# A hybrid decoder step on one core: first input chunk sent earlier, value rows and pooling maps interleaved anew, copy parts moved, last expert in pieces

## The reference

```
h = rms(x); q, k, v, u = split(h @ w_in)          # 12 heads x 64 each, u has 1280 channels
attn = dilated window attention(q, k, v, caches)  # samples read a window cache of 2048 rows
pool = (trailing mean of u over 2/4/8/16 rows - u) @ pool_w, scaled
x += concat(attn, pool) @ w_out
x += cross_attention(rms(x) @ w_cq, memory keys and values) @ w_co
group = top1(rms(x) @ w_rg + b_rg); experts = top2 of the group's 8 (w_re, b_re)
x += sum over the 2 experts: gate * ((silu(h @ w_e_gate) * (h @ w_e_up)) @ w_e_down)
```

## Time and profile before

| | us |
|---|---|
| median of 3 runs (lowest, highest) | 1586.22 (1583.8, 1587.32) |
| the profiled execution | 1590.57 |
| its span in the trace | 1588.7 |
| TensorE busy | 1260.9 |
| VectorE busy | 501.4 |
| ScalarE busy | 193.5 |
| bytes moved by DMA | 608.83 MB, 383 GB/s over the span |
| chain that ended last | DMA 50%, TensorE 43%, VectorE 3% |

### The profile page before, as it was taken

The page is one execution under the profiler, slowest core; times in us unless marked ns, Lnnn a source line. Parts: engine busy times, 40 slices in busy tenths (PEclk is TensorE's granted clock), DMA queues, the critical chain, the costliest instruction groups (busy, mean ns, idle before and its releaser), DMA issues.

```text
span 1588.7 us, 23505 instructions
## 1 busy us (share of the span) xinstructions
PE 1260.9 (79%) x10063; PEld 654.6 (41%) x10063; DVE 501.4 (32%) x1042; ACT 193.5 (12%) x464; POOL 59.6 (4%) x111
## 2 busy tenths in 40 slices
PE   7969999998999989676777677677677676676675
PEld 4434458773887866322222222222222222222222
DVE  2300155740000342442332332332332332332333
ACT  3200012320111134100000000000000000000000
POOL 2000012212000000000000000000000000000000
PEclk9989999997899999899889899899898998999898
DMA  9999999979899885699999999999999999999996
GB/s 358 339 370 332 331 348 375 390 226 366 308 395 407 333 339 216 285 398 426 425 427 428 424 428 426 424 427 427 424 428 428 423 429 426 424 429 426 426 427 259
DMA packets 113181, 608.83 MB, mean 383 GB/s; under 512 B 11118, under 2 KB 14341, under 8 KB 78681
## 3 DMA queue, kind: packets, MB, share of 16 engines
q1 hardware_dynamic: 71243, 479.10, 73.1%
q10 hardware_dynamic: 34486, 100.73, 17.4%
q0 software_dynamic: 7408, 28.37, 5.0%
HBM read 603.16 MB, written 106.18 MB: 446 GB/s over the span
## 4 chain that ended last, share of the span: by engine, by line
DMA 50%; PE 43%; DVE 3%; issue 2%; SPq 1%; ACT 1%; POOL 0%; DVEq 0%; ACTq 0%
DMA ring<-in_w_e_up_dram 44%; PE pb L1108 11%; PE pb L642 10%; PE pb L881 6%; DMA ring<-in_w_in_dram 3%; PE pb L728 2%; PE pb L1008 2%; PE pb L899 2%; PE pb L670 2%; DMA ring<-in_w_cq_dram 2%; PE pb L849 1%; PE pb L648 1%; DMA ring<-Z 1%; SPq L486 1%; PE pb L859 1%
## 5 line engine op out<-in xcount | busy, mean ns | idle before, releaser
L1108 PE MATMUL pb<-ring,xT 128*32 128x256 f32 x4096 | 312.4, 473 | 198.6 <-DMA ring<-in_w_e_up_dram 197.8
L1108 PEld LDWEIGHTS pb<-ring,xT 128*32 128x32 f32 x4096 | 155.2, 134 | 378.9 <-DMA ring<-in_w_e_up_dram 245.4
L1948 DVE TENSOR_TENSOR Z<-pb,Z 128x512 f32<-128x512 f32 x256 | 158.4, 680 | 343.8 <-PE pb L1072 343.8
L642 PE MATMUL pb<-ring,hreg 128*128 128x512 f32 (+1 forms) x320 | 127.4, 558 | 13.9 <-issue 13.9
L1135 PE MATMUL pb<-ring,xT 128*32 128x512 f32 x992 | 113.9, 600 | 0.0
L1072 PE MATMUL pb<-xT 32*128 32x512 f32 (+1 forms) x768 | 106.2, 623 | 3.7 <-DVE Z L1948 2.6
L1048 PE MATMUL pb<-Z,xT 128*32 128x512 f32 (+1 forms) x768 | 95.3, 610 | 3.0 <-DVE xT L1926 3.0
L642 PEld LDWEIGHTS pb<-ring,hreg 128*128 128x128 f32 x320 | 61.1, 193 | 77.1 <-issue 75.4
L881 PE MATMUL pb<-hreg,ring 128*128 128x264 f32 x320 | 78.1, 402 | 2.8 <-DMA ring<-in_w_out_dram 2.8
L728 PE MATMUL pb<-hreg,ring 128*128 128x264 f32 x320 | 76.2, 398 | 5.1 <-DMA ring<-in_w_in_dram 5.1
L1450 ACT ACTIVATE xT<-pb 128x128 f32<-128x128 f32 x32 | 8.9, 277 | 526.8 <-PE pb L1108 526.8
(11 more groups left out here) (323 smaller groups left out, 1122.6 us busy)
## 6 DMA issues: line engine op xcount, KB each, us to landing
ring<-in_w_e_gate_dram SPq DMA_DIRECT2D x64, 2048.0 KB, 19.0
ring<-in_w_e_up_dram SPq DMA_DIRECT2D x64, 2048.0 KB, 23.5
ring<-in_w_e_down_dram SPq DMA_DIRECT2D x31, 4096.0 KB, 22.1
out_win_k_sample_dram<-in_cache_win_k_dram ACTq DMA_DIRECT2D x24, 1536.0 KB, 12.9
out_win_v_sample_dram<-in_cache_win_v_dram ACTq DMA_DIRECT2D x24, 1536.0 KB, 14.9
ring<-in_w_in_dram SPq DMA_DIRECT2D x7, 4096.0 KB, 30.8
ring<-in_w_out_dram SPq DMA_DIRECT2D x4, 4096.0 KB, 32.1
out_win_k_sample_dram<-in_cache_win_k_dram ACTq DMA_DIRECT2D x8, 1488.0 KB, 14.9
```

Of the source, the lines that this page charges most:

```text
L642: last = mm(bk[:, 0:n], xt[:, k, tile * P:tile * P + P], w[:, k, 0:n], start=(k == 0), stop=(k == KT - 1))
L1108: last = mm(pb[1][32 * c:32 * c + 32, 0:256], XT[:, k % 4, 32 * (k // 4):32 * (k // 4) + 32], w[:, :, k8, P * c:P * c + P], start=(k == 0) ...
L1948: last = V.tensor_tensor(d, banks[c][:, :], d, ALU.add)
```

## The change

- SyncE sends the first chunk of w_in before it waits for the bias rows, not behind the load of their table.
- TensorE: the small matmuls on the pooling state come before the last channel tile (`channels(9)`), not behind it; the last channel rows are turned behind the first sample's value matmuls. The maps stand in front of the value matmuls of samples 1 to 7, two of them before 3, 4 and 6, where one stood behind each sample and two at the end. VectorE waits for the turned rows where it writes over the last two tiles.
- ScalarE: five copy parts fewer ahead of the output projection (one before the first input chunk, one each at the second and third, one at the last channel tile, one at the maps), the others at the maps later; one more in cross attention, one more in the last projection, and three behind the last exponential of the routing.
- The last expert: the second half of gate and up is loaded as two quarters, down as four (by column half, then by inner half); TensorE starts each when its piece is there. The down product goes to two banks by column half, each is copied and added to x by itself, and SyncE stores each piece of the prompt when it is final. ScalarE stores the sample rows. The branch for more blocks stands before the last expert.

```diff
+            big(IN0)
             sp.wait_ge(v_freed, v_at("bias", 0))
             sp.dma_start(bias_dram[:, :], brow[0:H, :]).then_inc(brow_stored, 16)
...
-            big(IN0)
             big(IN0 + 1)
...
-            with sp.Fori(2, NE) as i:
+            with sp.Fori(2, NE - 1) as i:
                 expert_weights(i, i)
+            sp.wait_ge(gu_used[0], NE - 1)
+            gate_up(NE - 1, NE - 1, 0)
+            sp.wait_ge(gu_used[1], NE - 1)
+            for q in range(2):
+                for m in range(2):
+                    src = a[("w_e_gate", "w_e_up")[m]][0][NE - 1].rearrange("(p k) n -> p k n", k=KT)
+                    at = 4096 * m + 2048 * q
+                    sp.dma_start(ring[:, 1, at:at + 2048].rearrange("p (k n) -> p k n", k=4), src[:, 8 + 4 * q:12 + 4 * q, :])\
+                        .then_inc(gu_landed[1] if q else quarter_landed, 16)
+            sp.wait_ge(dn_used, NE - 1)
+            w = a["w_e_down"][0][NE - 1].rearrange("(k p) n -> p k n", p=P)
+            for q in range(4):
+                c, f = slice(1024 * (q // 2), 1024 * (q // 2) + 1024), slice(2 * (q % 2), 2 * (q % 2) + 2)
+                sp.dma_start(slot2.rearrange("p (k n) -> p k n", k=4)[:, f, c], w[:, f, c]).then_inc(last_landed[q], 16)
...
+            for n, t, hf in ((1, 0, 0), (2, 1, 0), (3, 0, 1), (5, 1, 1)):
+                c = slice(1024 * hf, 1024 * hf + 1024)
+                sp.wait_ge(x_final, n)
+                sp.dma_start(a["y_prompt"][0, t * P:(t + 1) * P, c], x3[:, t, c]).then_inc(stored, 16)
...
-            channels(9)
-            channel_rows(8, 10)
...
-            piece_landed(pe, POOLW)
             pe.wait_ge(state_landed, 16)
...
+            channels(9)
...
+            sample_values(0)
+            channel_rows(8, 10)
+            piece_landed(pe, POOLW)
+            kt = 0
+            for b in range(1, NB):
+                for _ in range(2 if b in (3, 4, 6) else 1):
+                    pool_map(kt)
+                    kt += 1
+                sample_values(b)
...
+            def results(hf):
+
+                for t in ((0, 1), (0, 2, 1))[hf]:
+                    if t == 2:
+                        pe.wait_ge(x_final, 1)
+                    for c in range(4) if t == 2 else (2 * hf, 2 * hf + 1):
+                        r = slice(32 * c, 32 * c + 32)
+                        out = (pb[4 + c][:, :], pb[c][:, :], pb[4][32 * c:32 * c + NB, :])[t]
+                        last = mm(out, GT[r, slice(P * t, P * t + P) if t < 2 else slice(SEQ, TOK)], yo[r, :], start=True, stop=True)
+                    last.then_inc(out_filled, 1)
...
-            cache_part(3)
+            cache_part(2)
...
-                cache_part((2, 3, 3, 1, 0)[n])
+                cache_part((2, 2, 2, 1, 0)[n])
...
-                if o in (0,5,10):
+                if o in (0, 3, 6, 9):
                     cache_part()
...
+            cache_part(3)
+            assert parts == 8 * NB, parts
...
+                act.wait_ge(dn_used, NE)
+                nc.scalar.copy(yo[0:64, :], pb[3][0:64, :]).then_inc(yo_ready, 1)
+                act.wait_ge(dn_used, NE + 1)
+                nc.scalar.copy(yo[64:P, :], pb[2][64:P, :]).then_inc(yo_ready, 1)
+            act.wait_ge(x_final, 4)
+            for c in range(4):
+                act.dma_start(a["y_sample"][:, 0, 512 * c:512 * c + 512], x3s[32 * c:32 * c + NB, :]).then_inc(stored, 16)
```

More of the change, by code:

```diff
@@ L851, in pool_map, with sample_values @@
                 last.then_inc(a_filled, 1)
-            pe.wait_ge(a_freed, a_at("sturn", 1))
             sv = vbank("svals")
-            for b in range(NB):
+            def sample_values(b):
                 val_ready(pe, b)
@@ L1263, in channels @@
                 if j not in (0, 6):
[L1264 removed]
+                    cache_part()
             def channel_rows(first, end):
@@ L1436, in _ @@
             rows_back(3)
-            assert parts == 8 * NB, parts
             act.wait_ge(exp_in, 1)
@@ L1456, in expert @@
                 nc.scalar.copy(GT, pb[2][:, 0:TOK]).then_inc(gt_ready, 1)
-                act.wait_ge(dn_used, i + 1)
-                nc.scalar.copy(yo, pb[3][:, :]).then_inc(yo_ready, 1)
+                if not last_of_all:
+                    block_out(i)
             rows_out(0)
@@ L1948, in add_results, with results @@
                     last = V.tensor_tensor(d, banks[c][:, :], d, ALU.add)
-                    if final and c == 1:
-                        last.then_inc(x_final, 1)
-                last.then_inc(x_final if final else y_added, 1)
+                last.then_inc(y_added, 1)
+            def results():
+                for n, (hf, t) in enumerate(((0, 0), (0, 1), (1, 0), (1, 2), (1, 1))):
+                    dve.wait_ge(out_filled, n + 1)
+                    if t == 2:
+                        last = V.tensor_tensor(x3s, pb[4][:, :], x3s, ALU.add)
+                    for c in (2 * hf, 2 * hf + 1) if t < 2 else ():
+                        d = x3[:, t, 512 * c:512 * c + 512]
+                        last = V.tensor_tensor(d, pb[c if t else 4 + c][:, :], d, ALU.add)
+                    last.then_inc(x_final, 1)
             def expert(i, last_of_all=False):
@@ L1984, in _ @@
             n_over = dve.value_load(ov_i[0:1, OVB:OVB + 1], min_val=0, max_val=OVB)
-            expert(NE - 1, last_of_all=True)
             with dve.If(n_over > 0):
-                choose(NE)
-                rows_in(NE)
-                with dve.Fori(NE, NBLK) as i:
+                with dve.Fori(NE - 1, NBLK) as i:
                     expert(i)
-                for t in range(3):
-                    add_results(NBLK, t, pb[0:4] if t == 1 else pb[4:8], final=True)
             with dve.Else():
-                for t in range(3):
-                    add_results(NE, t, pb[0:4] if t == 1 else pb[4:8], final=True)
+                expert(NE - 1, last_of_all=True)
+            results()
 _INS = ['x_prompt', 'x_sample', 'cache_win_k', 'cache_win_v', 'state_pool', 'cache_mem_k', 'cache_mem_v', 'mem_prompt',
```

108 lines of the change are left out of this document (64 added, 44 removed).

## The result

| | before | changed |
|---|---|---|
| median of 4 runs each (lowest, highest) | 1585.01 (1583.3, 1587.32) | 1569.09 (1560.86, 1574.13) |
| the profiled execution | 1590.57 | 1574.13 |
| its span | 1588.7 | 1572.3 |

A forecast was written before the change was run, and what follows sets the result against it. Expert stage bound by bytes, mostly TensorE with four holes ahead of it. Gains 16.0 + 13.5 − 1.0 + 9.5 = 38.0 us take the profiled 1590.57 to 1552.6, the median from 1586.22 to 1548.2; range for 8 in 10: 1539 to 1566.

The forecast's parts named there:

- The early gain: First w_in chunk sent ahead of the bias rows, removing TensorE's wait: 16.0 us gained, bounds 7.7 and 16.0.
- covered, but with nothing to spare: Second w_in chunk: sent no earlier than 85, needed about 117, leaving 32 us, where w_out chunks land in 32.1.
- rival A: Early wait comes back at the second input chunk or the slowest one: 16 us lost, total 1564; chance 0.13.
- The middle: Value rows and pooling maps woven differently, removing waits and low-clock time: 13.5 us gained, bounds 5.6 and 19.4.
- B: Clock stays low in the woven stage: 9 us lost instead of 13.5 gained, total 1571; chance 0.11.
- D: Output projection starves as w_out chunks and w_cq meet a full queue: 59.6 us lost, total 1608; chance 0.05.
- a condition for the rest: Five copy parts fewer before the output projection free 18.3 us of engines, so the shortened stretch fits: 37 against 29.5.
- Routing: Three copy parts behind the last exponential, ending at 657 near the experts' first loads: 1.0 us lost, bounds 0 and 11.0.
- One sign of failure: The forecast fails as a whole if the expert loads start later than 645; they were expected near 629.
- The tail: Last expert loaded and finished in pieces: 9.5 us gained; lower bound the 1.9 of sample stores, upper 11.
- C's fixed cost: Last expert's smaller loads, 10 for 5, each pay about 2.0 us in series: total gain 28.5, time 1558; chance 0.08.
- The sum: Whole kernel: 16.0 + 13.5 − 1.0 + 9.5 = 38.0 us gained, for a median of 1548.2.

The follow-up runs named there:

- three profiles: The unaltered changed kernel, profiled once in each of three groups of runs; spans 1572.3, 1552.1 and 1569.9 us.
- second profile: The changed kernel again, unaltered, on another chip: span 1552.1 us; its group's median 1562.71 beside 1590.92 for the kernel before.
- first profile: The unaltered changed kernel as first measured: profiled execution 1574.13 us, span 1572.3; median 1569.09 beside 1585.01 for the kernel before.
- the third: The changed kernel once more, unaltered, on its own chip: span 1569.9 us; its group's median 1569.73 beside 1587.19 for the kernel before.
- the old order: TensorE's value rows and maps as before: in the changed kernel, median 1566.94 us; also in the kernel before with only w_in's first chunk moved ahead, 1579.97.
- the three groups: Runs of the unaltered changed kernel beside the kernel before: medians 1569.09 against 1585.01, 1562.71 against 1590.92, 1569.73 against 1587.19 us.
- parts behind the table: The changed kernel, with two of ScalarE's copy parts waiting until the bias table has landed: median 1557.49 us, ratio 0.9780 to the kernel before.
- three edits: The changed kernel with two copy parts waiting for the bias table, four parts later and the last down quarter before the first results: median 1558.26 us, ratio 0.9809.
- the first edit alone: The kernel before with only the first w_in chunk moved ahead of the bias rows: median of twelve 1579.97 us beside 1588.61, ratio 0.9949.

## Why the prediction was right or wrong

**The early gain, 16.0 predicted, is the step that failed.** It was 2.2, 16.3 and 5.8 in the three profiles and 11.6 between medians. The first chunk came out as forecast in the three. (The kernel before was profiled only at the lower level, 0.55 from 53 to 60 us; 2.2 and 5.8 compare the upper level with it, 16.3 like with like.) The step that failed is the one on what is moved past: "covered, but with nothing to spare". I took 32 us for the second chunk from w_out chunks, and called the store and the table covered since the table isn't needed for 60 us. But the store's 30.6 us hold back the table, and the table is what stands ahead of the second chunk in the queue. When the two leave decides how they fare against two copy parts, and the chunk took 46.2, 31.8 and 42.5 us in the three profiles. Nor does it hold that the chunk can't go before 85: it went at 83.0 and 81.9 at the upper level, yet landed later. With "nothing to spare" in the text, rival A should have had near half of the chance, not 0.13, and the range more room above. A's number, 1564, is near the three medians, but it has the 16 us lost always and to full engines; they are lost in some executions and kept in others.

**The middle, 13.5 predicted.** The stretch from the first value matmul to the first output tile took 51.4 us, and 40.4, 38.0 and 38.4 now: 11.1 to 13.5 less. The low clock behind the last values is gone (0.94 over the second profile's stretch), and B did not come as a whole: in the first profile 18 map records took 8.49 us at 371.0, at a clock of 0.51 from 371 to 379, where the second has 4.74. Two waits over 2 us stay, 2.31 in the second profile and 2.24 in the third, before the last value matmuls. D did not come: from the first output tile to w_cq it took 131.4, 129.3 and 131.4 us, 129.0 before. But the old order took 46.7 and 43.3 in two other profiles, so some 5 to 8 us of it are what that one execution had drawn; between means (47.1 of three profiles, 38.9 of the changed kernel's three) the order gives 8.2. That the gain against that one execution is near 13.5 is in part luck. The parts moved away carry another 9.2 between medians, which the prediction had as a condition for the rest and gave no price.

**Between the output projection and the experts** nothing was predicted to be lost. The second profile loses 1.2 us there; the first 4.3 (16.7 to 12.4), in w_cq's load (TensorE waits 6.03 us before its first use, 0.54 before the change) and in matmuls behind it at the lower level: 16.41 us for the first 64 records where before and the quickest profiles have 14.5.

**Routing, −1.0 predicted.** The lead shrinks by 0.7, 0.3 and 1.3 us from expert 0 to expert 1. That is right: the parts, with full engines from 639 to 651 us where before had none at 651, still run into the first loads. One sign of failure came true all the same: the first profile's flood of expert loads starts at 646.1, past the 645 that the prediction set (627.8 in the second, 643.8 in the third; 658.4 before).

**The tail, 9.5 predicted, 5.9 measured** (4.8 in the first profile). The answer to the earlier trace rows there; the first row is what stands behind the last gate and up matmuls:

```profile
1552.07 2.11 PE L1090 MATMUL pb<-xT 32*128 32x512 f32 x16
...
1555.64 3.66 PE L1116 MATMUL pb<-ring,xT 128*32 128x512 f32 x24
1560.04 1.99 PE L1110 MATMUL pb<-xT 32*128 32x512 f32 x8 [0.73 <-ACT xT L1525]
1561.96 1.91 PE L1116 MATMUL pb<-ring,xT 128*32 128x512 f32 x8
1564.55 3.16 PE L1110 MATMUL pb<-xT 32*128 32x512 f32 x16 [0.68 <-ACT xT L1527]
```

```profile
1563.91 0.58 ACT L1527 COPY xT<-pb 64x512 f32<-64x512 f32 x1 [4.02 <-PE pb L1116]
```

I put the copy of the second half 8.0 us behind the gate and up matmuls (1563.3 to 1571.3); it comes 11.8 behind (1552.1 to 1563.9). From it to the end I had 7.6, and it is 8.4. These 4.6 us are what is missing in this profile. The quarter is in TensorE's list behind the first results and their wait for the copy, 2.7 us that I had let run beside it. C's fixed cost is not seen: no wait of TensorE for a piece is over 1.4 us. The 2.0 us of the Trainium skill (DMA: Bandwidth & Descriptors, Anatomy of one DMA) are stated there for the path of GpSimd; SyncE issues these pieces, and no run here measures that cost.

**The sum.** For an execution in which the table leads, 36.6 against 38.0, and that by luck in part: the tail is 3 short, and the old kernel's profile was a poor one in the middle. For the median, 15.9, 28.2 and 17.5 in the three groups. With the order fixed it is 32.9 (parts behind the table) and 28.9 (three edits), so the race looks like the larger part of what is missing in the first and third group, and not all of it. That the other runs of the unaltered kernel split as their profiled ones do is inferred; they have no profile. The 3.2 us that the prediction took as what a measurement can tell were too small: the changed kernel's runs lie 13 to 21 us apart. Why the clock from 53 to 60 us falls now on one level and now on the other, and why the kernel before itself spreads over more than 20 us in each later group, stays open.

## What to carry to other kernels

A small store whose confirmation something waits for can take as long as what stands ahead of it in its queue: before moving a large load forward, follow every DMA that it is moved past to the next load that its waiter holds back. Where two queues fill the engines, give the load that is waited for a lead by a semaphore, rather than let the order of issue fall as the clock has it. And a cover "with nothing to spare" holds in some executions and not in others; it is to be priced as such.

## What the runs showed of the hardware

- An 18 KB store behind a 4 MB load in one queue took 30.6 us in the first profile and 27.9 to 35.7 in the eleven that have this order, until the next DMA left; 6.4 and 9.7 with none ahead of it, and 5.6 in another queue beside the same load. It isn't strictly first in, first out: in ten of the eleven it came between 2.6 us before the chunk's landing and 0.4 behind it, in the one with the first edit alone 6 us before.
- With engines full from two queues, a lead of 4.5 us (the table over the parts) went with 66.9% for SyncE's queue from 82 to 94 us, one of 0.9 us with 39.4%, and 1.0 us behind with 14.1%.
- TensorE's clock at one place differs between executions of equal code: from 53 to 60 us it was 1.00 in 7 of the 14 profiles and 0.51 to 0.60 in 7. Where the first chunk goes early and the order is open, the upper level came with 8 to 18 us of holes (5 profiles) and the lower with 0 to 2 (4 profiles).
